# Expert layer of a hybrid encoder: gate and up sums in three pairs of PSUM banks, bf16 casts on ScalarE

## What is computed

```python
def one_expert(args):
    xc, wg, wu, wd = args          # 160 x 1024; 1024 x 2048 twice; 2048 x 1024
    a = xc @ wg
    b = xc @ wu
    return (jax.nn.silu(a) * b) @ wd

ye = lax.map(one_expert, (xe, w_gate_e, w_up_e, w_down_e))
ye = ye * gates[..., None].astype(ye.dtype)
return jnp.zeros_like(h).at[idx.reshape(-1)].add(ye.reshape(-1, D))
```

## Time and profile before

| | before |
|---|---|
| median of 3 runs | 2915.61 us (2912.18 to 2917.41) |
| span of the profiled execution | 2913.2 us |
| TensorE busy | 2660.3 us, 91% |
| VectorE busy | 1681.9 us, 58% |
| ScalarE busy | 1229.0 us, 42% |
| GpSimd busy | 903.3 us, 31% |

### The profile page before, as it was taken

One profiled execution on the slowest core, in us unless ns is written; L12 is line 12 of the kernel. 1 busy time (PEld: TensorE's weight loads), 2 busy tenths in 40 slices (PEclk: granted clock), 3 DMA queues, 4 the chain that ended last, 5 costly groups with the idle time before them and its releaser, 6 DMA issues.

```text
span 2913.2 us, 46659 instructions
## 1 busy us (share of the span) xinstructions
PE 2660.3 (91%) x17898; PEld 2197.9 (75%) x17898; DVE 1681.9 (58%) x2075; ACT 1229.0 (42%) x1685; POOL 903.3 (31%) x352
## 2 busy tenths in 40 slices
PE   7999999999999999479989899998999999899997
PEld 4456677676777768368888888888888888888887
DVE  3011422432110143677987887797788779778876
ACT  2011333332000021145665565566566556656554
POOL 0004111110111000234344444434444443443443
PEclk9999999999999999789999999999999999999999
DMA  7211010010110143347787787778778777877872
GB/s 234 40 27 40 17 34 21 6 36 4 40 43 22 29 178 125 144 149 255 266 269 250 258 265 250 258 269 266 249 257 278 250 249 269 268 253 252 287 249 68
DMA packets 340356, 489.78 MB, mean 168 GB/s; under 512 B 22090, under 2 KB 194777, under 8 KB 340192
## 3 DMA queue, kind: packets, MB, share of 16 engines
q1 hardware_dynamic: 332864, 461.60, 46.9%
q0 software_dynamic: 7328, 25.58, 4.1%
HBM read 462.28 MB, written 24.87 MB: 167 GB/s over the span
## 4 chain that ended last, share of the span: by engine, by line
PE 62%; issue 23%; DVE 11%; ACT 2%; DMA 1%; SPq 0%; DVEq 0%; POOL 0%; ACTq 0%; POOLq 0%
PE ps L1267 28%; PE ps L1524 15%; PE ps L1527 7%; PE ps L1447 4%; PE ps L1372 3%; DVE gu L1200 2%; DVE act_f L1207 2%; PE ps L1385 2%; DVE w_lo L434 1%; DVE act_b L1213 1%; DVE act_hl L1215 1%; ACT w_hi L855 1%; PE ps L1514 1%; PE ps L1332 1%; DMA spos_s_sb<-in_spos_s 1%
## 5 line engine op out<-in xcount | busy, mean ns | idle before, releaser
L434 POOL TENSOR_TENSOR w_lo<-raw,w_hi 128x2048 bf16<-128x2048 f32 x132 | 635.5, 4816 | 800.7 <-ACT w_hi L855 800.7
L1524 PE MATMUL ps<-x_hl,w_hi 128*128 128x320 f32 x4112 | 755.9, 327 | 128.4 <-issue 78.3
L855 ACT ACTIVATE w_hi<-raw 128x2048 fp32r<-128x2048 f32 x388 | 739.2, 1906 | 3.0 <-issue 3.0
L1524 PEld LDWEIGHTS ps<-x_hl,w_hi 128*128 128x128 f32 x4112 | 630.2, 195 | 146.0 <-issue 82.6
L434 DVE TENSOR_TENSOR w_lo<-raw,w_hi 128x2048 bf16<-128x2048 f32 x256 | 624.8, 2441 | 96.0 <-ACT w_hi L855 96.0
L1527 PE MATMUL ps<-x_b,w_lo 128*128 128x160 bf16 x4112 | 382.6, 237 | 0.0
L1524 PE MATMUL ps<-act_hl,w_hi 128*128 128x320 f32 x2048 | 349.0, 322 | 0.0
L1527 PEld LDWEIGHTS ps<-x_b,w_lo 128*128 128x128 bf16 x4112 | 279.0, 100 | 54.0 <-issue 3.2
L1524 PEld LDWEIGHTS ps<-act_hl,w_hi 128*128 128x128 f32 x2048 | 311.9, 194 | 2.0
L1207 DVE TENSOR_TENSOR act_f<-silu,gu 128x160 f32<-128x160 f32 x256 | 213.7, 835 | 19.4 <-ACT silu L880 19.4
L873 ACT ACTIVATE lows<-ps 128x320 f32<-128x320 f32 x256 | 111.0, 434 | 254.9 <-PE ps L1527 253.7
(11 more groups left out here) (179 smaller groups left out, 2997.0 us busy)
## 6 DMA issues: line engine op xcount, KB each, us to landing
raw<-in_w_g SPq DMA_DIRECT2D x64, 2048.0 KB, 9.0
raw<-in_w_u SPq DMA_DIRECT2D x64, 2048.0 KB, 11.4
raw<-in_w_d SPq DMA_DIRECT2D x64, 2048.0 KB, 9.1
m_raw<-in_w_in SPq DMA_DIRECT2D x16, 512.0 KB, 4.7
h_raw<-in_w_in SPq DMA_DIRECT2D x12, 512.0 KB, 4.0
x_in<-in_x SPq DMA_DIRECT2D x10, 512.0 KB, 4.2
x_res<-in_x SPq DMA_DIRECT2D x10, 512.0 KB, 4.1
y_out<-x SPq DMA_DIRECT2D x10, 512.0 KB, 2.9
```

What stands on the lines that cost most here:

```text
L434: engine.tensor_tensor(unit(w_lo, v), raw_half(v), unit(w_hi, v).bitcast(F32), ALU.subtract)\
L855: act.activation(unit(w_hi, w), raw_half(w), ACT.Copy).then_inc(hi_ready, 1)
L1524: pe.matmul(out, unit(w_hi, v)[:, k, cols], hl[:, k, :, :].rearrange("p a n -> p (a n)"), start=k == 0, stop=False)
```

## The change

Four things. The pairs of banks for gate and up become three (0, 2 and 6 and their neighbours, j % 3), and TensorE starts tile j when `gu` of tile j-3 is made; for that the third group of transposed tokens goes to bank 2 in place of 0, the first rows of the output to banks 3 and 0 in place of 1 and 2, and the wait for the last scaled rows stands ahead of tile 2 in place of the transposes. The casts to `x_b` and `act_b` go from VectorE to ScalarE, with semaphores of their own (`xb_ready`, `act_b_ready`), on which TensorE, and VectorE ahead of writing `act_f` again, wait. GpSimd gives its credit for the first units behind their low parts in place of ahead. The split of low parts between VectorE and GpSimd stays.

```diff
-X_BANKS = ((6, 0, 3), (7, 3, 3), (0, 6, 2))
-Y_BANKS = ((1, 2), (6, 7))
+X_BANKS = ((6, 0, 3), (7, 3, 3), (2, 6, 2))
+Y_BANKS = ((3, 0), (6, 7))
+GU_BANKS = (0, 2, 6)
...
-            pool.sem_inc(lo_pool, sum(v in POOLS for v in range(LEAD)))
             for v in range(LEAD):
                 low_part(pool, 0, v, first_units)
+            pool.sem_inc(lo_pool, sum(v in POOLS for v in range(LEAD)))
...
             def token_high(n):
                 act.wait_ge(xf_ready, n + 1)
                 act.activation(x_hl[:, :, 0, :], x_f[:, :, :], ACT.Copy).then_inc(x_hi_ready, 1)
+                act.activation(x_b[:, :, :], x_f[:, :, :], ACT.Copy).then_inc(xb_ready, 1)
...
                 def low_sums(j):
 
-                    b = 2 * (j % 2)
+                    b = GU_BANKS[j % 3]
...
                     act.activation(act_hl[:, 2 * pair:2 * pair + 2, 0, :], act_f[pair % 2][:, :, :], ACT.Copy)\
                        .then_inc(act_hi_ready, 1)
+                    act.activation(act_b[:, 2 * pair:2 * pair + 2, :], act_f[pair % 2][:, :, :], ACT.Copy)\
+                       .then_inc(act_b_ready, 1)
...
                 op.then_inc(xf_ready, 1)
-                dve.wait_ge(xf_ready, n + 1)
-                dve.tensor_copy(x_b[:, :, :], x_f[:, :, :])
...
-                        dve.wait_ge(act_hi_ready, e * 8 + (j // 2 - 1))
+                        dve.wait_ge(act_b_ready, e * 8 + (j // 2 - 1))
...
                     dve.wait_ge(act_f_ready, e * FT + (2 * pair + 2))
-                    dve.tensor_copy(act_b[:, pairs, :], act_f[pair % 2][:, :, :])
...
                 for j in range(1, FT):
-                    if j >= 2:
-                        pe.wait_ge(gu_added, e * FT + (j - 1))
+                    if j == 2:
+                        pe.wait_ge(y_ready, e * 4 + 1)
+                    if j >= 3:
+                        pe.wait_ge(gu_added, e * FT + (j - 2))
                     tile_of_gate_and_up(e, j)
                 pe.wait_ge(gu_added, e * FT + (FT - 1))
-                pe.wait_ge(y_ready, e * 4 + 1)
                 pe.wait_ge(rows_moved, e * 64 + 64)
                 expert_transposes()
...
                             pe.wait_ge(act_ready, e * 8 + k1 // 2)
+                            pe.wait_ge(act_b_ready, e * 8 + k1 // 2)
...
                 pe.wait_ge(x_ready, e + 2)
+                pe.wait_ge(xb_ready, e + 2)
```

More of the change, by code:

```diff
@@ L75 @@
 RAW_SLOTS, UNIT_SLOTS, LEAD = 4, 6, 4
+POOLS = [v for v in range(UNITS) if v % 3 == 2]
+DVES = [v for v in range(UNITS) if v % 3 != 2]
 def place_of(v):
@@ L86, in ahead @@
     return [2 * step + LEAD, 2 * step + LEAD + 1] if step < 8 else [step + 8 + LEAD]
-POOLS = [v for v in range(UNITS) if v % 3 == 2]
-DVES = [v for v in range(UNITS) if v % 3 != 2]
 def attention_tiles():
@@ L388, in build @@
         x_ready = sem("x_ready")
+        xb_ready = sem("xb_ready")
+        act_b_ready = sem("act_b_ready")
         gu_ready = sem("gu_ready")
@@ L1199, in add_lows @@
                     dve.wait_ge(low_ready, e * FT + (j + 1))
-                    dve.tensor_tensor(gu[j % 2][:, :, :], gate_up(2 * (j % 2))[:, :, 0:CAP], lows[j % 2][:, :, :],
+                    dve.tensor_tensor(gu[j % 2][:, :, :], gate_up(GU_BANKS[j % 3])[:, :, 0:CAP], lows[j % 2][:, :, :],
                                       ALU.add).then_inc(gu_added, 1)
@@ L1544, in _ @@
             pe.wait_ge(x_ready, 1)
+            pe.wait_ge(xb_ready, 1)
             tile_of_gate_and_up(0, 0)
```

## The result

| | before | after |
|---|---|---|
| median of the runs compared, 4 each | 2916.51 us (2912.18 to 2918.04) | 2936.69 us (2934.90 to 2938.34) |
| ratio, 95% interval | | 1.0067 [1.0053, 1.0081] |
| span of the profiled execution | 2913.2 us | 2933.9 us |
| mean granted clock of TensorE | 0.956 | 0.948 |
| TensorE / VectorE / ScalarE / GpSimd busy | 2660.3 / 1681.9 / 1229.0 / 903.3 us | 2685.0 / 1598.1 / 1280.4 / 891.7 us |

The change makes the kernel 20 us slower. The forecast was 2910, with "faster" as the likeliest sign. TensorE is 25 us busier, and no matmul was added: that points to the clock.

A forecast was written before the change was run, and what follows sets the result against it. A chain of GpSimd, VectorE and ScalarE was taken to bound the gate/up part, TensorE trailing. 37.4 + 6.7 - 32.0 - 6.8 = 5.3 us gained, 2910 us for the median; range 2876 to 2937.

The forecast's parts named there:

- "faster" as the likeliest sign: Whole kernel: chance 0.47 of faster than 2909.8 us, against 0.28 for the same and 0.25 for slower.
- The gate/up part: From the loop's turn to the transposes: 2.34 us shorter per expert, 37.4 us over 16, with 1.5 us of waiting left.
- Two terms of the sum: Gate/up chain, sum 1.54 us: act_b's 0.40 on ScalarE within a 0.36 gain; GpSimd's low parts 0.21 shorter, twice.
- the low clock behind the loop's turn: Behind the 5 us of issue at the turn: 6.8 us at the low level, no change counted.
- The 3.9 us: TensorE's waits for the sum gu in the gate/up part, per expert: what a third pair of banks can give.
- The collision of `x_hl`: Down part: x_hl starts 0.3 us behind GpSimd and stands still; new yT wait 1.7 us, cost 2.0 per expert, 32 us.
- yT freed of `x_b`: Down part: yT of tile 0 no longer queued behind x_b; 0.84 us in 8 of 16 experts, 6.7 us gained.
- The clock: Behind the transposes: falls in 12 experts of 16 instead of 8, 4 x 1.7 = 6.8 us lost.
- The price of one fall: Low clock behind the transposes: up to half of 3.4 us, 1.7 us for each fall.
- The halfway choice: Count of experts whose clock falls behind the transposes: 12, chosen halfway between 8 and 16.
- The slower rival of 2937 us: Clock also falls behind the new 1.7 us wait ahead of tile 3's transposes: 16 x 1.7 = 27 us, 2937; 17%.
- the forecast's own case: Whole kernel: the summed terms hold, 2910 us, from 2898 to 2922, clock falls behind the transposes; 53%.

The follow-up runs named there:

- the kernel with the casts alone: The kernel before, still with two pairs of banks, but the casts to x_b and act_b on ScalarE: 2935.87 us, 1.0071 of before.
- the idle time filled: The changed kernel plus 12 unused matmuls of down tile 0 ahead of the wait for tile 14's sum: 2917.17 us, 1.0006 of before.
- the run with the order mended and the casts on VectorE: Changed kernel, first 12 of 16 products of down tile 0 ahead of the transposes, x_hl ahead of unit 22's low part, casts back on VectorE: 2912.31 us.
- with the order mended: First products of down tile 0 ahead of the transposes and x_hl early: changed kernel 2861.29 us; with casts on VectorE 2912.31, with two pairs 2911.40.

## Why the prediction was wrong

**The gate/up part: right, in part by luck.** It foretold 2.34 us less per expert and one wait of 1.5 us ahead of the transposes; measured 2.31 and 1.5. In the expert of the earlier trace rows the transposes start 62.79 us behind the last back (1879.04, 1941.83), before 65.05 (1873.60, 1938.65). Two terms of the sum can be read off and held: `act_b` on ScalarE pushes the next instruction back by 0.36 us, where 0.40 was taken, and GpSimd's low parts take a mean of 4.66 us over the program in place of 4.82.

But the low clock behind the loop's turn, which the prediction took as it was, became shorter: 6.8 us in all 15 turns of before, now 6.8 in 6 of them and 3.4 in 9. The second 3.4 us behind two turns of the changed kernel, in the columns of the earlier trace rows:

```profile
1886.40:1889.80 3.40, 3.40 (x19) 3.20 (x19) 0.00 (x0) 0.00 (x0) 3.40 (x2) 0.50 1.08 278
1992.20:1995.60 3.40, 3.30 (x27) 2.87 (x27) 0.49 (x1) 1.49 (x2) 3.40 (x2) 1.00 0.91 187
```

From the turn to the transposes the 6 take 62.96 us and the 9 62.13. With the clock at the turn as before, the part is therefore 1.81 us shorter and not 2.34, and by the 0.85 us of the one expert read in the earlier trace rows the sum of tile 14 comes 1.0 us earlier in place of 1.54; which of the terms fell short is not shown. The 1.5 us of waiting came out right for a like reason. The 3.9 us that it was worked out from are the weight loads' row; TensorE's matmuls themselves waited 48.8 / 16 = 3.1 us per expert:

```profile
PE ps L1524 <- DVE gu L1200: 48.8, 64, 1.2
```

Both terms were too large by half a microsecond or more, and their difference was right. Why the turn's stretch became shorter is open.

**The collision of `x_hl`: right.** A wait of 1.8 us in each expert in place of 1.7; first to fourth back 1.94 us longer in place of 2.0. The cast to `x_b` on ScalarE took 1.16 to the next instruction, against 1.17 taken from the row of `x_hl`.

**yT freed of `x_b`: right in its place, but worth nothing here.** Before, TensorE waited for yT at the first back in experts without a fall:

```profile
1949.96 0.33 PE L1562 MATMUL ps<-ident,yT 128*128 128x128 f32 x1 [0.54 <-DVE yT L1222]
```

At 1955.44 in the changed kernel it does not wait. Without a fall, the stretch from the transposes to the first back was 11.31 us before and is 10.60 in the kernel with the casts alone: 0.71 of the 0.84 foretold. In the changed kernel every expert falls, so none of them shows the gain.

**The clock: the step that failed.** The prediction took "12 experts of 16, chosen halfway between 8 and 16", 4 falls more at 1.7 us each, 6.8 us. All 16 fall, and 13 of them for 6.8 us. The stretch from the transposes to the first back had been expected to stay as it was (6.7 us gained by yT, 6.8 lost by the clock) and grew by 24.5 us; with the 5.7 of yT (8 x 0.71) that the stretch would have given without falls, the clock cost some 30 us in place of 6.8. The price of one fall was right: with the casts alone the stretch takes 10.60 us in the 11 experts without a fall and 12.16 in the 5 with one of 3.4 us, 1.56 more where 1.7 was taken. What failed is the count, four falls more than the 12 (4 x 1.56 = 6 us), and above all the length: in the changed kernel the stretch takes 12.21 us with a fall of 3.4 us and 13.46 with one of 6.8, and the difference for 13 experts is another 16 us. The mean clock agrees: (1 - 0.956) x 2913.2 x 2 = 256 us at the low level before, (1 - 0.948) x 2933.9 x 2 = 305 after, 49 us more, which can cost half of that, 24.5. (The shorter low clock behind 9 turns gives back 9 x 0.83 = 7.5 us, and so the count behind the transposes alone comes out higher.) The mechanism was named, and its size was wrong in two ways: how often, and how long. The halfway choice rested on two rows (3.4 us of transposes alone, and waits of 1.4 us between dense matmuls), and neither showed the two joined together.

**The slower rival of 2937 us came to the right number for the wrong reason.** It had the clock fall behind the new wait for yT. That wait is 1.8 us long and stands between dense matmuls (the wide ones of the down tiles, one right behind the other), and the clock behind it is 1.00 in the windows above and in every expert. The falls lie behind the transposes, where the forecast's own case put them. What the rival supposed does happen behind a longer wait for yT, the 2.6 us ahead of the first back in three experts of the run with the order mended and the casts on VectorE.

**The sum.** Gate/up part, yT and collision together gained 37.0 + 5.7 - 31.0 = 11.7 us, 7.5 of it by the clock at the turn; the clock's 30 behind the transposes and 0.8 in the rest made that 19 lost.

## What to carry to other kernels

A wait is not priced by its length alone: look at what the engine does right behind it. 1.5 us of standing joined to a run of small transposes brought the clock down in every expert, mostly for twice as long as before, and 1.8 us between dense matmuls cost nothing but itself (2.6 us there did bring it down); work that can already run (here 12 products of the next tile) belongs in the gap. And two edits that each made the kernel 18 and 20 us slower alone (three pairs, the casts moved), and with the order mended gave 4 to 5 us, can be worth 50 us more together once what they collide with is moved out of the way, so a change that comes out slower is taken apart before it is dropped.

## What the runs showed of the hardware

- Clock: in three kernels with 1.5 to 2.4 us of idling directly ahead of 3.4 us of transposes, and in the changed one, the granted clock fell to 0.5 in 16 of 16 experts, for 6.8 us in most and up to 10.2; with the same transposes and no idling just ahead of them it fell in 3 to 13 experts, depending on the kernel, mostly for 3.4 us. Standing of 1.8 us between dense matmuls brought no fall; standing of 2.6 us between them brought one in each of the 3 experts that had it. From the transposes to the first back a fall of 3.4 us cost 1.56 us, one of 6.8 us 3.0 (10.65 and 13.63 with the idle time filled).
- TensorE can gain from work that nobody uses: 12 matmuls more per expert made the changed kernel 20 us faster.
- VectorE and GpSimd: with a start 0.40 us behind GpSimd's, `x_hl` takes 5.65 us; two places earlier in the queue it takes 1.49. Between the first back and the fourth that order is worth 2 us per expert.
